# Gate blocks of the delta mixer moved among the sample heads, a shorter first inverse level, and the router's products joined in columns

## What is computed

```python
proj = h @ w_in                     # layer 0: q, k, v (18 blocks of 128 columns), z (6), b, a, memory queries (2)
qkv, conv_new = short_conv(proj[..., :o1], conv_prev, conv_w)
q, k = l2norm(q), l2norm(k)         # per head
o, s_new = gated_delta_rule(q, k, v, g, beta, s_prev)   # 512 tokens in chunks, triangular inverse; 8 tokens in one step
o = rmsnorm(o, g_onorm) * jax.nn.silu(z)                # z: the gate
x = x + concat([o, mem_attend(mq, mk, mv)]) @ w_out
...                                 # dense FFN; layer 1: latent attention, then the experts:
probs = jax.nn.softmax(h @ w_router)                    # 8 experts
top_p, top_i = lax.top_k(probs, 2)  # each token goes to two experts
```

## Time and profile before

| what | us |
|---|---|
| runs | 2356.29, 2355.93, 2352.83; median 2355.93 |
| profiled execution, whole / span | 2352.37 / 2350.4 |
| PE busy / DVE / ACT / POOL over the span | 2162.8 / 695.3 / 513.9 / 244.3 |
| projection stage, from the end of its first block (66.4 to 258.5) | 192.1 |
| chunk stage (267.5 to 460.1) | 192.6 |
| sample stage (460.1 to 579.4) | 119.3 |
| router, from the end of the last norm to the first expert block (1575.6 to 1632.0) | 56.4 |

### The profile page before, as it was taken

How to read it: one execution, slowest core, us unless ns; L and a number is a source line. 1 busy time by engine, 2 the same in 40 slices (tenths; PEclk the granted TensorE clock), 3 DMA queues, 4 the chain that set the end, 5 groups by cost and what they waited for, 6 DMA issues and landing times.

```text
span 2350.4 us, 35462 instructions
## 1 busy us (share of the span) xinstructions
PE 2162.8 (92%) x14771; PEld 1936.5 (82%) x14771; DVE 695.3 (30%) x1341; ACT 513.9 (22%) x1100; POOL 244.3 (10%) x325
## 2 busy tenths in 40 slices
PE   7999889898899999988998999986999999999991
PEld 6888688867799999987656766776999999999991
DVE  3355656463242222232254444121000000000003
ACT  3344322320132122121242333012011111101101
POOL 0100201011023113100300332001000000000001
PEclk9999999955999999999987999786999999999996
DMA  8322000130223324150802664206898899889773
GB/s 229 98 69 66 11 1 4 37 119 36 63 73 103 93 84 122 38 151 0 280 2 71 225 231 174 81 1 170 212 276 202 207 235 244 207 206 277 203 187 121
DMA packets 452949, 306.21 MB, mean 130 GB/s; under 512 B 22381, under 2 KB 435456, under 8 KB 448704
## 3 DMA queue, kind: packets, MB, share of 16 engines
q1 hardware_dynamic: 433812, 225.85, 37.1%
q0 software_dynamic: 19024, 78.72, 9.9%
HBM read 276.53 MB, written 28.14 MB: 130 GB/s over the span
## 4 chain that ended last, share of the span: by engine, by line
PE 88%; DVE 6%; issue 2%; DMA 1%; ACT 1%; POOL 1%; SPq 0%; POOLq 0%; DVEq 0%; ACTq 0%
PE bank L1320 18%; PE bank L549 16%; PE bank L1349 9%; PE bank L966 5%; PE bank L970 5%; PE bank L968 5%; PE bank L1160 3%; PE bank L757 2%; PE bank L742 2%; PE bank L752 1%; PE bank L1174 1%; PE bank L1201 1%; PE bank L896 1%; PE bank L827 1%; PE bank L1052 1%
## 5 line engine op out<-in xcount | busy, mean ns | idle before, releaser
L1320 PE MATMUL bank<-arena,w_ring 128*128 128x176 f32 x2816 | 424.6, 314 | 4.8 <-issue 4.8
L1320 PEld LDWEIGHTS bank<-arena,w_ring 128*128 128x128 f32 x2816 | 422.5, 191 | 6.8 <-issue 6.8
L549 PE MATMUL bank<-hT,w_ring 128*128 128x260 f32 x1440 | 326.5, 389 | 6.6 <-DVE hT L1381 5.5
L549 PEld LDWEIGHTS bank<-hT,w_ring 128*128 128x128 f32 x1440 | 278.1, 194 | 51.3 <-issue 7.2
L1991 ACT ACTIVATE arena<-bank 128x512 f32<-128x512 f32 (+5 forms) x286 | 135.5, 493 | 483.3 <-PE bank L549 190.1
L1349 PE MATMUL bank<-arena 128*128 128x176 f32 x1408 | 219.6, 313 | 0.0
L1349 PEld LDWEIGHTS bank<-arena 128*128 128x128 f32 x1408 | 210.2, 190 | 0.0
L1953 DVE TENSOR_TENSOR arena<-arena,bank 128x176 f32<-128x176 f32 x88 | 29.7, 338 | 431.6 <-PE bank L1320 431.6
L966 PE MATMUL bank<-hH,gu_high 128*128 128x260 f32 x704 | 143.0, 284 | 7.6 <-DVE hL L1372 7.6
L970 PE MATMUL bank<-hH,w_low 128*128 128x260 f32 x704 | 142.3, 284 | 0.0
L968 PE MATMUL bank<-hL,gu_high 128*128 128x260 f32 x704 | 142.3, 284 | 0.0
(11 more groups left out here) (465 smaller groups left out, 2847.6 us busy)
## 6 DMA issues: line engine op xcount, KB each, us to landing
w_ring<-in_we_gate SPq DMA_DIRECT2D x88, 512.0 KB, 7.2
w_ring<-in_we_up SPq DMA_DIRECT2D x88, 512.0 KB, 7.3
arena<-in_we_down SPq DMA_DIRECT2D x64, 704.0 KB, 6.5
w_ring<-in_w_in_a SPq DMA_DIRECT2D x26, 512.0 KB, 3.9
w_ring<-in_w_gate SPq DMA_DIRECT2D x22, 512.0 KB, 3.9
w_ring<-in_w_up SPq DMA_DIRECT2D x22, 512.0 KB, 3.9
arena<-in_w_down SPq DMA_DIRECT2D x16, 704.0 KB, 6.2
slots<-arena POOLq DMA_DIRECT2D x4, 2560.0 KB, 21.7
```

What stands on the lines that cost most here:

```text
L549: mm = pe.matmul(out[i][:, 0:hi - lo], w_ring[:, s, kt, :], rhs[:, kt, lo:hi], start=(kt == 0), stop=(kt == KT - 1))
L1320: mm = pe.matmul(bank[bk][:, 0:SLOTS], w_ring[:, s, kt, :], hTe[:, kt, :], start=(kt == 0), stop=(kt == KT - 1))
```

## The change

- The six gate blocks leave the projection stage. They run in the sample stage as `gate_block`, each in two halves of four k-tiles: gate 0 around the first memory scores, gates 1 to 4 in heads 0 to 3, gate 5 in two halves after head 5. They use banks 6 and 7 alone, the rest of the stage takes turns on six. ACT applies silu in place in PSUM (`head_gate`), DVE multiplies it into the head. `zs` is gone; the mixer's output has a tile of its own (`mix0`), since the gate blocks still read `hT`.
- `LENGTH_AT` brings all twelve lengths into blocks 3 to 17.
- `head_sums` comes ahead of head 0 (squares in `Vb0`, so the memory values are loaded after it), `head_roots` by the table `NORM_AT`.
- Level 0 of the inverse has no products but a transpose: `Einv` is picked from `LT`, `Dinv` from its transpose.
- Router: the router's columns are stationary (32 columns, four k-tiles side by side in the array), `hT` moves; ACT copies, PE turns, DVE adds the four strips. The counts take 6 products in place of 20. The router's weights are loaded into `wba` after the dense part.

```diff
-LENGTH_AT = [6, 9, 12, 15] + [QKV + i for i in range(2 * H - 4)]
+LENGTH_AT = [3, 4, 5, 7, 8, 9, 11, 12, 14, 15, 16, 17]
+NORM_AT = [[], [], [0], [1], [2, 3], [4]]
+IN_A_ORDER = [i for i in range(QKV)] + [QKV + H, QKV + H + 1]
...
-            for blk in range(QKV + H + 2):
-                weights_block(pe, ("a", blk), hT, HALVES)
+            for blk, at in enumerate(IN_A_ORDER):
+                weights_block(pe, ("a", at), hT, HALVES)
...
+                            if lv == 0:
+                                mm = pe.transpose(b[:, cc], LT[:, i, cc], ident)
+                            else:
+                                mm = pe.matmul(b[:, cc], LT[:, i, cc], Dinv[:, i, cc], start=True, stop=True)
                         mm.then_inc(full(("X", h, lv)), 1)
+                    if lv == 0:
+                        continue
...
+            def gate_block(h, first, last):
+
+                if first == 0:
...
+                    pe.wait_ge(w_loaded[s], 16 * (n + 1))
+                    for hf in range(2):
+                        claim(pe, (("a", QKV + h), hf), (w_used[s], n + 1), pinned=6 + hf)
+                    gate_slot[h] = s
+                s = gate_slot[h]
+                for kt in range(first, last):
+                    for hf, (lo, hi) in enumerate(HALVES):
+                        mm = pe.matmul(bank_of((("a", QKV + h), hf))[:, 0:HALF], w_ring[:, s, kt, :], hT[:, kt, lo:hi],
+                                       start=(kt == 0), stop=(kt == KT - 1))
+                if last == KT:
+                    mm.then_inc(w_used[s], 1)
...
+            lanes[0] = 6
+            gate_block(0, 0, KT // 2)
             memory_queries(0)
             memory_scores(0, 0)
+            gate_block(0, KT // 2, KT)
+            head_sums()
             for i in range(H):
                 delta_read(i)
+                if i + 1 < H - 1:
+                    gate_block(i + 1, 0, KT // 2)
                 if i + 1 < MH:
                     memory_scores(0, i + 1)
                 delta_turn(i)
...
+                if i + 1 < H - 1:
+                    gate_block(i + 1, KT // 2, KT)
                 delta_write(i)
...
+            gate_block(H - 1, 0, KT // 2)
             memory_row_weights(0)
+            gate_block(H - 1, KT // 2, KT)
+            head_roots(H - 1)
             sample_norm()
...
+                        if lv == 0:
+
+                            dve.copy_predicated(out=Einv[:, i, :].rearrange("p (c i) -> p c i", c=NT),
...
+                            pick(("X", h, 0), Dinv[:, i, :], 0)
+                            continue
...
+            def head_gate(h):
+
+                b = filled(act, (("a", QKV + h), 0))
+                act.activation(b[:, 0:HALF], b[:, 0:HALF], ACT.Silu)
+                b = filled(act, (("a", QKV + h), 1))
+                act.activation(gsamp[:, h, :], b[:, S - HALF:HALF], ACT.Silu)
+                act.activation(b[:, 0:S - HALF], b[:, 0:S - HALF], ACT.Silu).then_inc(gate_silu, 1)
...
+            parts = [claim(pe, ("rt4", hf)) for hf in range(2)]
+            for k in range(2):
+                pe.wait_ge(h_ready, 4 * KT + QUADS * (k + 1))
+                for hf, (lo, hi) in enumerate(HALVES):
+                    for j in range(QUADS):
+                        mm = pe.matmul(parts[hf][32 * j:32 * j + 32, 0:HALF], wba[:, QUADS * k + j, :], hT[:, QUADS * k + j, lo:hi],
+                                       start=(k == 0), stop=(k == 1), skip_group_check=True)
...
+                    pe.matmul(b[:, 0:6 * NE], incl, chosen, start=True, stop=False, skip_group_check=True)
+                    for t in range(1, NT + 2):
...
+            weights([("a", i) for i in IN_A_ORDER[3:]])
+            weights([("a", QKV + h) for h in range(H)])
+            weights([("o", 0, i) for i in range(5)])
```

More of the change, by code:

```diff
@@ L1263, in _ @@
             stream_sum(NORM_FFN1, 4 * KT + 5, sqx[1])
-            pe.wait_ge(h_ready, 5 * KT)
-            pe.wait_ge(late_in, 64)
-            b = claim(pe, "rt")
[L1267 to L1271, removed]
+            pe.wait_ge(small_in, 64)
+            parts = [claim(pe, ("rt4", hf)) for hf in range(2)]
[5 more added lines that the diff above has]
+                                       start=(k == 0), stop=(k == 1), skip_group_check=True)
+                    if k == 1:
+                        mm.then_inc(full(("rt4", hf)), 1)
+            for hf in range(2):
+                freed(pe, ("rt4", hf))
+            b = claim(pe, "rt")
+            for t in range(NT):
+                mm = pe.transpose(b[:, t * P:(t + 1) * P], router_parts[:, t * P:(t + 1) * P], ident)
             mm.then_inc(full("rt"), 1)
+            b = claim(pe, "rts")
+            pe.transpose(b[0:NB, 0:P], router_parts[:, S:T], ident).then_inc(full("rts"), 1)
             for name, src in (("ht", hT), ("xt", xT)):
@@ L1285, in _ @@
                     b = claim(pe, "upto")
[L1286 to L1290, removed]
+                    pe.matmul(b[:, 0:6 * NE], incl, chosen, start=True, stop=False, skip_group_check=True)
+                    for t in range(1, NT + 2):
+                        n = min(t + 5, NT + 2)
+                        mm = pe.matmul(b[:, t * NE:n * NE], ones, chosen[:, 0:n - t, :], start=False, stop=(t == NT + 1),
+                                       skip_group_check=True)
                     mm.then_inc(full("upto"), 1)
@@ L2122, in _ @@
                     act.activation(kgs[:, h, :], kgt, ACT.Exp).then_inc(dt_exp, 1)
-                for lv in range(LEVELS):
+                for lv in range(1, LEVELS):
                     for i, h in enumerate(heads):
@@ L2602, in _ @@
             load(lmw.bitcast(I32), a["const_masks"], masks_in)
-            load(wrt, rows(a["w_router"][0]), late_in)
             sp.dma_start(g_on, a["g_onorm"].rearrange("l p -> p l"),
@@ L2634, in _ @@
                 delta_load(h)
-                if h % 2:
-                    for n in range(4 * (h // 2 - 1), 4 * (h // 2)):
-                        memory_row(0, n, True)
+            filled(sp, "osum")
+            for n in range(NB):
+                memory_row(0, n, True)
+            weights([("o", 0, i) for i in range(5, KT)])
             def dense_mixer(name, parts, wg, wu, wd):
@@ L2660, in _ @@
             sp.wait_ge(d_used[DS - 1], loops["dense"][2][DS - 1] + 2 * DENSE_PARTS)
+            load(wba[:, :, 0:NE], rows(a["w_router"][0]), small_in)
             load(cs, a["const_rope"].rearrange("p (a t) -> p a t", a=2), rope_in)
```

126 lines of the change are left out of this document (74 added, 52 removed).

## The result

| kernel | runs, us | median | ratio to before, 95% interval |
|---|---|---|---|
| before, runs beside it | 2356.29, 2355.93, 2352.83, 2353.81 | 2354.87 | |
| changed | 2321.66, 2313.91, 2316.71, 2319.29 | 2318.0 | 0.9844 [0.9824, 0.9863] |

The change made the kernel 36.9 us faster, 1.6%. The forecast was 2312 with a range from 2297 to 2331. The execution that was profiled is the slowest of the four (2321.66), and that of before (2352.37) lay 2.5 under the median, so the two traced executions are only 30.7 us apart, 30.3 by their spans.

What follows compares the result with a forecast made beforehand. PE was taken to set the time nearly everywhere, at a low clock in the sample stage and router. Terms -42 - 2 - 3 - 13 + 18 = -42 took 2352.4 to 2310, the runs' median 2355.9 to 2314; forecast 2312, range 2297 to 2331.

Steps and rivals of the forecast that it cites:

- Step 1: Projection stage: six gate blocks of 7.01 us leave a stage that is all PE, 42 us less; 0 to 12 lost.
- The first sign of being right: Projection stage 42 us shorter at PEclk near 1, without PE gaps ahead of L677.
- It fits, with 0.9 to spare: Projection stage: DVE's 7.0 us for convolution and length fit in a block of PE's 7.01 plus 0.88.
- the lengths don't fit: Rival, projection stage: PE stalls in blocks 5 to 17, +12 us, 2324; chance 0.09 together with the router rival.
- Steps 2 and 3: Projection stage's end: 2 of PE's 6.87 us wait gained; level 0 of the inverse: 3 us less for both groups.
- Step 4: Router: stationary columns save 10 us, fewer count products 3, so 13 us less; bounds 8 to 14.
- Step 5: Sample stage: with the six gate blocks it grows by 18 us, from 119.3 to 137.6; bounds +2 to +82.
- the 6 taken: Sample stage: the clock falls in two of four gaps between heads, at 3.5 us each, +6.
- 9 were taken: Sample stage: waits of 9 us, about 4 at the end, 2 in heads 4 and 5, 3 behind the sixth gate block.
- the step's other terms: Sample stage: 104.6 us all high, +9 heads 4 and 5, +7 memory values, +2 gate 5, +6 clock falls.
- The prediction's reading of the low stretch: Sample stage, 470 to 495: busy PE at 1.2 GHz on products of 2 columns or 8 or 64 rows; wide products raised it.
- the rival by which it stays low throughout: Sample stage: the clock stays low despite the gate blocks, +82 us there, time 2375; chance 0.06.

Runs made afterwards that it cites:

- experiment 1: Changed kernel with no length in block 4 (second length at block 5, third at 7, block 10 used instead): 2309.48 us, ratio 0.9799.
- experiment 4: Changed kernel with level 0 of the inverse as before (products X, Y and Z, ACT's copy, two picks): 2322.91 us, ratio 0.9855.
- experiment 6: Kernel before with only the router of the change (columns stationary, counts in six products): 2340.51 us, ratio 0.9936.
- Experiment 3: Changed kernel with two of the eight k-tiles of each gate block, so its output isn't the reference's: 2305.26 us, ratio 0.9792.
- experiment 5: Changed kernel with each gate block whole, at the place of its second half: 2330.78 us, ratio 0.9889.
- experiment 2: Changed kernel with the sixth gate block inside head 4 in place of two halves behind head 5: 2313.85 us, ratio 0.9821.
- experiment 7: Changed kernel with no length in block 4 and with the sixth gate block in head 4: 2306.02 us, ratio 0.9792.
- experiment 8: Against experiment 7, gate i stands in head i for all six heads: 2310.01 us, ratio 0.9802.

## Why the prediction was right

Taken by its own steps:

- **Step 1, six gate blocks out of the projection stage, was mis-sized**: 42 forecast, 30.7 measured in the stage (192.1 less 161.4). The first sign of being right, no PE gaps at PEclk near 1, did not come. "It fits, with 0.9 to spare" compared the busy time of DVE and ACT with a block of PE. That held: experiment 1 puts six lengths in a row without a wait. (The 5.6 us for ACT don't follow from 77.2 over 26 blocks and one load, which is 4.3, but a block with two loads does keep ACT busy for about 5.4.) What it left out is how long a bank is held: the time from PE's sum to ACT's root, a whole block later by ACT's order, in a round of eight. The loss lies within the bounds of this step (0 to 12) and was the rival "the lengths don't fit", +12, right in size; but that one spoke of stalls spread over blocks 5 to 17, and it is two waits in one place, with a slow block behind each.
- **Steps 2 and 3** gave 6.3 for 5. The wait of 6.87 before the first row product fell to 0.15, more than the 2 taken for it, but most of that comes back, since the third head now waits for DVE and then runs low (in experiment 4 it waits 5.3 us, and its first products take 2.07 in place of 1.12). From the turns of the convolution state to the first Y of level 1 it was 37.26 us before and is 35.15 in experiment 4, which has level 0 as before: 2.1 are left, so the 2 stands. Level 0 gave 4.6 (experiment 4).
- **Step 4, the router**, gave 14.3 for 13; alone 14.5 by the trace and 15.9 by the median (experiment 6).
- **Step 5, the sample stage**, came out at 137.6, as forecast, but its parts differ. Low starts of halves cost (5.46 + 5.46 + 6.30 - 3 x 3.75) = 6.0 ahead of gate 5, as the 6 taken, in three places and not two; gate 5's first half 2.0, as taken. Waits were 4.2 us (137.60 - 133.44) where 9 were taken, among other reasons because the silu behind gate 5 cost little, since its table was loaded while ACT waited for the block:

```profile
540.86 1.28 ACT L2244 ACT_TABLE_LOAD   x1
544.32 0.37 ACT L2244 ACTIVATE bank<-bank 128x260 f32<-128x260 f32 x1 [2.18 <-PE bank L924]
```

  The Trainium skill, "ScalarE: Activation LUTs", section "What ACT_TABLE_LOAD costs", counts a drain with each switch; the rows have the whole load ahead of a wait of 2.18, so neither the page's price nor the forecast's 1.28 was paid here.

  PE's busy time, 133.4, is longer than the 128.6 of the step's other terms by as much as the waits are shorter, so some of the work ran lower than thought; that the two misses cancel is luck. That wide blocks raise the clock for what stands beside them was the guess on which this step rested. The prediction's reading of the low stretch didn't show it: from 470 to 495 there are not only products of 2 columns or 8 to 64 rows but also turns with 128 rows and 128 columns, which ran low as well (about 1.1 at the high level):

```profile
479.73 1.97 PE L847 MATMUL bank<-CF,arena 128*128 128x128 f32 x8
```

  Experiment 3 does show it, and experiment 5 that the spacing counts too. The clock of 0.81 in the changed kernel refutes the rival by which it stays low throughout (2375).

By the traces, for which the sum of -42 was made, the change gave 30.7, so it is 11.3 short: the 11.4 of step 1 and the 1.9 ahead of its stage, less what steps 2 to 4 gave beyond their terms (2.6), the rest being under 1. The medians are 36.9 apart, 5 short, because the traced execution of the changed kernel is the slowest of four that spread over 7.8 us. So the mechanism of the sum held in all steps but the bank turn in step 1; that the time came within 6 us of 2312 owes part to that spread and to step 5's two misses.

What stays open: why a half block begins low in one execution and not in another, with the same instructions before it. So the 5 us of experiment 2 can't be called a gain for certain.

## What to carry to other kernels

When steps of several engines are set closer together, don't add up busy times alone: follow each shared buffer from its claim to its release, in the order of the engine that releases it, and count how many claims lie between in the round. Wide matmuls that must run somewhere can be worth most among narrow ones, in pieces with short gaps; in this stage their net price was about half of their own time (17.7 of 33.7 us). A wait on TensorE can cost more than itself: the waits of 2.35 and 4.33 us had a block behind them that ran partly at the low clock, 1.6 to 3.1 us longer.

## What was not expected of the hardware

- The same order of instructions gets its low stretches at different places. The changed kernel and experiment 1 have the same sample stage; in the first the second halves of gates 1 and 3 and the first halves of 4 and 5 began low, in the second the first halves of 2, 4 and 5. Experiments 2 and 7, alike there too, took 130.9 and 134.4 us. Why is open. The runs of the changed kernel spread over 7.8 us, those of before over 3.5.
- The clock can fall with TensorE busy. Behind 24 passes of 12 rows against 8 columns, 2.84 us long (L706), the next block takes 8.96 in place of 7.18 in experiment 1, with no wait ahead of either: the granted clock is 1.00 in the block ahead of L706, 1.00 in L706 and 0.50 in the first 3 us behind it. But this differs between executions too. Of the ten profiled, seven have a slow block there (9.0 to 10.2 us), and three, experiments 3, 5 and 8, have none, though others with the same instructions there do. So L706 alone does not decide it. Experiment 3, at 1.00 throughout:

```profile
123.40 2.84 PE L706 MATMUL bank<-rstd,sel 12*128 12x8 f32 x24
126.17 7.28 PE L552 MATMUL bank<-hT,w_ring 128*128 128x260 f32 x32
```
